# Moving half of the expert row sums from VectorE to ScalarE

## The chip, the cores and the metric

The kernel runs on one core of a Trainium2 chip. The metric is the device time of one execution in microseconds. TensorE does the matmuls (PE in the profile, its weight loads PEld), VectorE is DVE, ScalarE is ACT, GpSimd is POOL, and SyncE (SP) issues the plain weight transfers. Each has its own queue of instructions, worked off in order. They tell each other of finished work through semaphores.

## The reference, cut to what matters

The program is two layers over 256 tokens of width 1024, in float32. Each layer mixes tokens (a convolution, an attention and a state-space scan), attends to a memory, and ends in a feed-forward part that draws on a table of 16384 experts. The change touches that last part alone:

```python
# for each chunk of 128 tokens: 8 heads x 16 chosen experts per token
u_e = jnp.take(u_tab, expert, axis=0)
v_e = jnp.take(v_tab, expert, axis=0)
act = jax.nn.gelu(jnp.einsum('chkd,cd->chk', u_e, xc).astype(jnp.float32))
return jnp.einsum('chk,chkd->cd', (gate * act).astype(v_e.dtype), v_e)
```

So for each of 128 chosen experts of a token, a dot product of 1024 products (the `u` row with the token), a gelu, a gate factor, and a weighted sum of the `v` rows.

## The kernel before, in words

**Stages.** Tokens lie on the 128 partitions. There are four stages `ci`, two chunks of 128 tokens in each of two layers. The expert part of one stage overlaps with the mixing, memory attention and expert choice of the next. Experts are numbered `n` = 0 to 511, 128 in a stage. For each `n`, GpSimd issues one indirect gather (line 1145) that brings, for every token, the `u` row and the `v` row of one expert, 128 rows of 8 KB, into one of nine slots of `slots`. The `u` half is `slots[:, s, 0:D]`, the `v` half follows it.

**The path of one expert.** VectorE waits for the gather and makes the dot product (`dot_of`, line 2030): one instruction multiplies the `u` half by the token (`htok`), writes the products back into the slot, and adds them up into one column of `dot`; a second instruction reads the accumulator out. ScalarE takes two experts at a time (`gelu`, line 1534): it waits until both dots are there, makes one gelu of two columns, then two products with the gate (`coef`, line 1539), and then scales the identity by each coefficient (`diagonal`, line 1521). TensorE multiplies that diagonal with the `v` half, in two matmuls of 512 columns, and so adds the expert up in two PSUM banks (`add_expert`, line 1007). After the second matmul, the semaphore `slot_used` lets GpSimd gather the next expert into the slot. For 33 experts VectorE adds the `v` half up instead.

**What sets the order.** Every engine walks the same loop over ticks, one expert per tick from tick 100 on. All other work is written as strands, each piece with the tick at which it is issued. On ScalarE a tick does this in order: diagonals of the last pair (even `n`), strands of this tick, and on odd `n` the gelu of the pair `n-1, n`. VectorE's tick: the dot of `n`, then strands. TensorE runs two ticks behind. Different activation functions need a table load on ScalarE (ACT_TABLE_LOAD); it is put in front of the activation that needs it.

**Single experts.** The last four experts (`n` from `SINGLE` = 508) get a gelu each.

Of the kernel before, what the change touches and what calls it, by code (L numbers as in the profile page):

```python
# [10 lines left out]
ALU = mybir.AluOpType  # L11
ACT = mybir.ActivationFunctionType
# [5 lines left out]
D = 1024  # L18
# [13 lines left out]
PH, NK, TOP = 8, 128, 16  # L32
# [99 lines left out]
SINGLE = NG - 4  # L132
# [3 lines left out]
SLOT = [n % 7 for n in range(20)] + [(6, 8, 0, 1, 7, 2, 3, 4, 5)[n % 9] for n in range(NG - 20)]  # L136

USED = [SLOT[:n].count(SLOT[n]) for n in range(NG)]


def in_slot_before(n):

    return max(k for k in range(n) if SLOT[k] == SLOT[n])
# [7 lines left out]
def begun(pieces):  # L151

    return [[next(p, NEVER), p] for p in pieces]


def go_on(strands, tick):
    for s in strands:
        while s[0] <= tick:
            s[0] = next(s[1], NEVER)


def build(nc, x_d, mem_d, blocks_d, prm_d, rows_d, experts0_d, experts1_d, out_d):
    ctx = ExitStack()
    with ctx:
        def sb(name, shape, dt=F32):
            return ctx.enter_context(nc.sbuf_tensor(name, shape, dt))

        def sem(name):
            return ctx.enter_context(nc.semaphore(name))

        x = sb("x", [P, NC, D])
        slots = sb("slots", [P, SLOTS, 2 * D])
# [5 lines left out]
        htok = sb("htok", [P, 2, D])  # L178
# [71 lines left out]
        dot = sb("dot", [P, 2, TOP])  # L250
# [100 lines left out]
        gexp_ready = sem("gexp_ready")  # L351
        idx_ready = sem("idx_ready")
        dot_ready = sem("dot_ready")
        gelu_ready = sem("gelu_ready")
        gate_ready = sem("gate_ready")
        coef_ready = sem("coef_ready")
# [754 lines left out]
        def _(eng):  # L1111
# [17 lines left out]
            for n in range(NG):  # L1129
# [6 lines left out]
                s = SLOT[n]  # L1136
                if USED[n]:
                    before = in_slot_before(n)
# [12 lines left out]
        def _(eng):  # L1151
            act = nc.scalar.activation
# [15 lines left out]
            def root_ahead():  # L1168

                act(ahead[:, :], epsb[:, :], ACT.Sqrt)  # L1170
# [305 lines left out]
            def phasors(l):  # L1476
                at = BEGIN[l]
                for n, i in enumerate((1, 0)):
                    yield at + (15 + n if l == 0 else SETUP_TICK[1](ANGLE_OP[1]) + 1)
                    eng.wait_ge(angle_ready, 2 * l + n + 1)  # L1480
                    act(T[:, :, i, :], T[:, :, i, :], ACT.Sin, scale=TURN).then_inc(phasor_ready, 1)

            def gates():
                for q in range(NST * PH):
                    yield route_tick(q, BEST_OP) + (1 if q else 0)
                    j = q % 2
                    eng.wait_ge(best_ready, q + 1)
                    if q < len(HEADS[0]):
                        act(gexp[:, j, :], best[:, j, :], ACT.Exp, scale=rs0[:, :], bias=nbest[:, j, :],
                            accum_out=gsum[:, j, :]).then_inc(gexp_ready, 1)  # L1490
                        if q == 0:
                            act(ahead1[:, :], zero[:, :], ACT.Gelu_apprx_tanh)
                    else:
                        act(gexp[:, j, :], best[:, j, :], ACT.Exp, bias=nbest[:, j, :], accum_out=gsum[:, j, :])\  # L1494
                            .then_inc(gexp_ready, 1)

            def final(c):
                yield FINAL[c]
                root_ahead()
                for i in range(2):  # L1500
                    h = slice(i * 512, (i + 1) * 512)
                    eng.wait_ge(x_added, 2 * (NST - NC + c) + i + 1)
                    act(htok[:, 0, h], x[:, c, h], ACT.Square, accum_out=fss[:, i:i + 1]).then_inc(half_squared, 1)
                eng.wait_ge(half_squared, 2 * c + 2)
                eng.wait_ge(first_part, c + 1)
                act(root[:, :], fss[:, 1:2], ACT.Sqrt, scale=1.0 / D, bias=fpart[:, :]).then_inc(norm_root, 1)
                yield FINAL[c] + 2
                eng.wait_ge(final_rs, c + 1)
                b, n = turn[("gain", 1, ("final", c))]
                eng.wait_ge(emptied[b], n + 1)  # L1510
                act(outs[c][:, 512:], outs[c][:, 512:], ACT.Copy, scale=rs[:, :]).then_inc(out_right, 1)
                if c == NC - 1:
                    eng.wait_ge(out_right, c + 1)
                    nc.scalar.dma_start(out_d[c * P:(c + 1) * P, 512:], outs[c][:, 512:]).then_inc(stored, 16)

            def diagonal(n):
                q, k = divmod(n, TOP)
                i = TAKEN[n]
                if i >= DIAGS:
                    eng.wait_ge(slot_used, i - DIAGS + 1)  # L1520
                act(diag[:, i % DIAGS, :], ident[:, :], ACT.Copy, scale=coef[:, q % 2, k:k + 1])\  # L1521
                    .then_inc(diag_ready, 1)
# [5 lines left out]
            for l in range(L):  # L1528
                strands += [mem_keys(l), phasors(l)]
            strands = begun(strands + [gates()] + [final(c) for c in range(NC)])  # L1530
            def gelu(n, many):
                q, k = divmod(n, TOP)
                eng.wait_ge(dot_ready, n + many)
                act(gel[:, q % 2, k:k + many], dot[:, q % 2, k:k + many], ACT.Gelu_apprx_tanh).then_inc(gelu_ready, 1)  # L1534
                if k == 0:
                    eng.wait_ge(gate_ready, q + 1)
                eng.wait_ge(gelu_ready, n // 2 + 1 if many == 2 else SINGLE // 2 + n - SINGLE + 1)
                for i in range(k, k + many):
                    act(coef[:, q % 2, i:i + 1], gel[:, q % 2, i:i + 1], ACT.Copy, scale=gexp[:, q % 2, i:i + 1])\  # L1539
                        .then_inc(coef_ready, 1)  # L1540

            for tick in range(LAST):
                n = tick - G0
                if 2 <= n <= SINGLE and n % 2 == 0:
                    eng.wait_ge(coef_ready, n)
                    for k in (n - 2, n - 1):
                        if TAKER[k] == "tensor":
                            diagonal(k)
                if SINGLE < n <= NG:
                    eng.wait_ge(coef_ready, n)  # L1550
                    diagonal(n - 1)
                go_on(strands, tick)
                if 0 <= n < SINGLE and n % 2:
                    gelu(n - 1, 2)
                if SINGLE <= n < NG:
                    gelu(n, 1)

        @block.vector
        def _(eng):
            v = nc.vector  # L1560
# [464 lines left out]
            def dot_of(n):  # L2025
                q, k = divmod(n, TOP)
                ph = n // PER
                s = SLOT[n]
                eng.wait_ge(arrived[s], 16 * (USED[n] + 1))
                v.tensor_tensor_reduce(out=slots[:, s, 0:D], in0=slots[:, s, 0:D], in1=htok[:, ph % 2, :],  # L2030
                                       scale=1.0, scalar=0.0, op0=ALU.mult, op1=ALU.add,
                                       accum_out=dot[:, q % 2, k:k + 1]).then_inc(dot_ready, 1)
# [66 lines left out]
            for tick in range(LAST):  # L2099
                n = tick - G0  # L2100
                ph, m = divmod(n - PER - 2, PER)
                if m == 0 and 0 <= ph < NST:
                    add_to_x(ph)
                if 0 <= n < NG and n % TOP == 0:
                    gate_factor(n // TOP)
                if 0 <= n < NG:
                    dot_of(n)
                if 2 <= n <= NG + 1 and TAKER[n - 2] == "vector" and n % 2 == 0:
                    add_slot(n - 2)
                go_on(strands, tick)  # L2110
                go_on(route, tick)
                if 2 <= n <= NG and n % 2 == 0 and TAKER[n - 1] == "vector":
                    add_slot(n - 1)
# [7 lines left out]
def route_tick(q, n):  # L2121

    if q == 0:
        return 94
    if q == 1:
        return 97 + n * 3 // 4
    if q == PH * (NST - 1) or q % PH not in HEADS[q // PH]:
        return G0 + TOP * (q - 1) + 1 + (n - 1) // 2
    return G0 + TOP * (q - 1) - 6 + (n - 1)
# [78 lines left out]
```

## Time and profile before

| What | us |
|---|---|
| Median of the three runs | 1693.98 |
| The runs | 1693.75, 1693.98, 2640.91 |
| The profiled execution's own time | 1695.05 |
| Its span, first to last instruction | 1693.1 |
| Busy: TensorE 91%, VectorE 69%, ScalarE 43%, GpSimd 35% | |
| DMA over the span: 675.13 MB, mean 399 GB/s | |

The span is what the profile shows of one execution. A busy share is an average over stages that differ; what is worth something in one of them is read from that stretch. Idle time of an engine is put down to what ended it.

### The profile page before, as it was taken

What the parts mean: (1) busy time and instruction counts of PE and PEld (TensorE: products, weight loads), DVE (VectorE), ACT (ScalarE), POOL (GpSimd) and SP (SyncE); (2) the same over time, 40 slices, a digit from 0 to 9 for tenths busy, and PEclk for the clock granted to TensorE, in tenths of its full rate; (3) what the DMA queues carried; (4) which work ended last, traced back from release to release, by engine and by line L of the source; (5) the groups of instructions that cost most, each with busy time, mean ns of one, the idle gap of its engine ahead of it and who ended that gap; (6) DMA issues with size and microseconds to landing.
All of it is one profiled execution on the core that took longest, in us unless ns stands there. A gap on an engine that the chain in (4) does not pass through costs nothing.

```text
span 1693.1 us, 19218 instructions
## 1 busy us (share of the span) xinstructions
PE 1538.1 (91%) x6354; PEld 893.6 (53%) x6354; DVE 1170.7 (69%) x2955; ACT 734.0 (43%) x1963; POOL 595.9 (35%) x527
## 2 busy tenths in 40 slices
PE   9999999889999999988988889988999999777776
PEld 8757775347567656434645446434656554222232
DVE  7821899974877658986555667995556666666655
ACT  4142534763464333385433353465444334333333
POOL 0000454443333334343333343343343544344331
PEclk9999999999999999999999999999999999999999
DMA  9655999999999999999999999999999999999996
GB/s 384 258 201 221 381 416 421 421 422 420 421 420 420 421 414 421 420 419 421 420 421 421 411 421 421 380 416 412 421 410 419 421 420 421 421 422 421 421 421 285
DMA packets 94003, 675.13 MB, mean 399 GB/s; under 512 B 10424, under 2 KB 10704, under 8 KB 12496
## 3 DMA queue, kind: packets, MB, share of 16 engines
q0 software_dynamic: 73728, 536.90, 76.6%
q1 hardware_dynamic: 20032, 136.74, 20.0%
q8 instruction: 51, 0.84, 0.2%
q14 instruction: 48, 0.39, 0.1%
q10 hardware_dynamic: 144, 0.26, 0.0%
HBM read 672.81 MB, written 1.05 MB: 398 GB/s over the span
## 4 chain that ended last, share of the span: by engine, by line
PE 36%; DMA 34%; DVE 9%; ACT 5%; issue 2%; POOL 0%; DVEq 0%; ACTq 0%; POOLq 0%
DMA slots<-expert_rows,expert 34%; PE bank L1007 20%; PE bank L477 7%; DVE slots L2030 5%; PE bank L680 3%; PE bank L974 2%; PE bank L990 2%; ACT diag L1521 1%; ACT coef L1539 1%; ACT L1534 1%; PE bank L575 1%; PE bank L767 1%; PE bank L745 1%; ACT gel L1534 1%; DVE htok L1853 0%
## 5 line engine op out<-in xcount | busy, mean ns | idle before, releaser
L1007 PE MATMUL bank<-slots,diag 128*128 128x512 f32 x1914 | 899.7, 606 | 128.3 <-ACT diag L1521 121.5
L1145 POOL DMA_INDIRECT slots<-expert_rows,expert x512 | 593.9, 1160 | 1073.1 <-PE bank L1007 861.2
L2030 DVE CUSTOM_DVE_ANT_0 slots<-slots,htok 128x1024 f32<-128x1024 f32 x512 | 625.6, 1222 | 388.8 <-DMA slots<-expert_rows,expert 387.5
L1007 PEld LDWEIGHTS bank<-slots,diag 128*128 128x128 f32 x1914 | 345.4, 192 | 543.5 <-issue 321.7
L1534 ACT ACTIVATE gel<-dot 128x2 f32<-128x2 f32 (+1 forms) x258 | 52.5, 203 | 652.4 <-DVE dot L2030 651.7
L477 PEld LDWEIGHTS bank<-hT,ring 128*128 128x128 f32 x1488 | 180.6, 193 | 41.9 <-issue 40.4
L477 PE MATMUL bank<-hT,ring 128*128 128x128 f32 x1488 | 181.7, 276 | 1.4 <-ACT hT L1181 1.0
L1521 ACT ACTIVATE diag<-ident,coef 128x128 f32<-128x128 f32 x479 | 168.3, 394 | 8.8 <-PE bank L1007 0.4
L1539 ACT ACTIVATE coef<-gel,gexp 128x1 f32<-128x1 f32 x512 | 123.1, 287 | 10.4
L1534 ACT ACT_TABLE_LOAD x67 | 86.0, 1283 | 1.2
L1566 DVE SCALAR_TENSOR_TENSOR sg<-pad,prm,sg 128x128 f32<-128x128 f32 x240 | 71.5, 343 | 0.0
L680 PE MATMUL bank<-ring,hT 128*128 128x512 f32 x104 | 48.8, 598 | 1.0 <-issue 0.9
L1566 DVE SCALAR_TENSOR_TENSOR x<-slots,coef,x 128x1024 f32<-128x1024 f32 (+1 forms) x34 | 43.1, 1266 | 9.3 <-ACT coef L1539 9.2
L680 PE MATMUL bank<-ring,products 128*128 128x512 f32 x96 | 45.1, 592 | 0.0
L2030 DVE DVE_READ_ACCUMULATOR2_ANT dot<- 128x1 f32 x512 | 42.0, 82 | 0.0
L477 PEld LDWEIGHTS bank<-hT,slots 128*128 128x128 f32 x352 | 40.9, 192 | 2.1 <-issue 1.9
L477 PE MATMUL bank<-hT,slots 128*128 128x128 f32 x352 | 41.5, 275 | 0.3 <-DMA slots<-w_blocks 0.3
L477 PEld LDWEIGHTS bank<-hT,kept 128*128 128x128 f32 x256 | 31.6, 197 | 6.3 <-issue 6.3
L680 PEld LDWEIGHTS bank<-ring,hT 128*128 128x128 f32 x104 | 19.6, 193 | 26.1 <-issue 26.1
L1494 ACT ACT_TABLE_LOAD x25 | 32.1, 1283 | 0.4
L477 PE MATMUL bank<-hT,kept 128*128 128x128 f32 x256 | 31.7, 280 | 0.0
L536 PE MATMUL bank<-ring,hT 128*128 128x512 f32 x64 | 29.7, 592 | 0.0
(362 smaller groups left out, 1469.7 us busy)
## 6 DMA issues: line engine op xcount, KB each, us to landing
ring<-w_blocks SPq DMA_DIRECT2D x89, 1024.0 KB, 9.3
slots<-w_blocks SPq DMA_DIRECT2D x24, 1024.0 KB, 10.9
slots<-expert_rows,expert POOLq DMA_INDIRECT x512, 15.9
kept<-w_blocks SPq DMA_DIRECT2D x4, 1024.0 KB, 11.7
keys<-w_blocks SPq DMA_DIRECT2D x2, 1024.0 KB, 10.3
kv<-w_blocks SPq DMA_DIRECT2D x2, 1024.0 KB, 14.3
prm<-small SPq DMA_DIRECT2D x2, 768.0 KB, 12.9
x<-x_rows SPq DMA_DIRECT2D x2, 512.0 KB, 11.5
```

The costliest lines, as they stand in the source:

```text
L477: last = mm(bank[b][:, a * P:(a + 1) * P], w[:, k, a * P:(a + 1) * P], src[:, k, :], start=k == 0, stop=k == KT - 1)
L680: last = mm(bank[b + i][:, :], src[:, first + k, :], w[:, k, i * 512:(i + 1) * 512], start=start and k == 0, stop=stop and k == 1)
L974: last = mm(bank[b][:, a * M:(a + 1) * M], w[:, k, a * P:(a + 1) * P], memH[l][:, k, :], start=k == 0, stop=k == KT - 1)
L990: last = mm(bank[b][:, :], memH[l][:, t, m * P:(m + 1) * P], w[:, k, :], start=t == 0, stop=t == KT - 1)
L1007: last = mm(bank[h][:, :], diag[:, i % DIAGS, :], slots[:, SLOT[n], D + h * 512:D + (h + 1) * 512], start=m == 0, stop=n == end - (ph == N ...
L1145: nc.gpsimd.indirect_dma_start(slots[:, s, :], None, (experts0_d, experts1_d)[n // PER // NC], bass.IndirectOffsetOnAxis(ap=idx[q % 2][:, ...
L1494: act(gexp[:, j, :], best[:, j, :], ACT.Exp, bias=nbest[:, j, :], accum_out=gsum[:, j, :])\
L1521: act(diag[:, i % DIAGS, :], ident[:, :], ACT.Copy, scale=coef[:, q % 2, k:k + 1])\
L1534: act(gel[:, q % 2, k:k + many], dot[:, q % 2, k:k + many], ACT.Gelu_apprx_tanh).then_inc(gelu_ready, 1)
L1539: act(coef[:, q % 2, i:i + 1], gel[:, q % 2, i:i + 1], ACT.Copy, scale=gexp[:, q % 2, i:i + 1])\
L1566: return v.scalar_tensor_tensor(out=out, in0=in0, scalar=scalar, in1=in1, op0=op0, op1=op1)
L2030: v.tensor_tensor_reduce(out=slots[:, s, 0:D], in0=slots[:, s, 0:D], in1=htok[:, ph % 2, :], scale=1.0, scalar=0.0, op0=ALU.mult, op1=ALU.add,
```

## The change

Of each pair of experts that share a gelu, the first (even `n`, below 508, so 254 experts) is treated differently. VectorE only multiplies, with `tensor_tensor`, and writes the products into the slot. ScalarE then copies the 1024 products of each token onto themselves with an accumulator output, which puts their sum in the column of `dot`. A new semaphore `sum_ready` tells of it. The second expert of the pair and the last four are as before. The new step stands in ScalarE's tick `n`, behind that tick's strands; the strands of tick `n+1` and the pair's gelu come behind it.

```diff
+def summed_on_act(n):
+
+    return n % 2 == 0 and n < SINGLE
...
+            def sum_of_products(n):
+                q, k = divmod(n, TOP)
+                us = slots[:, SLOT[n], 0:D]
+                eng.wait_ge(dot_ready, n + 1)
+                act(us, us, ACT.Copy, accum_out=dot[:, q % 2, k:k + 1]).then_inc(sum_ready, 1)
+
             def gelu(n, many):
                 q, k = divmod(n, TOP)
+                if summed_on_act(n):
+                    eng.wait_ge(sum_ready, n // 2 + 1)
                 eng.wait_ge(dot_ready, n + many)
                 act(gel[:, q % 2, k:k + many], dot[:, q % 2, k:k + many], ACT.Gelu_apprx_tanh).then_inc(gelu_ready, 1)
...
                 go_on(strands, tick)
+                if 0 <= n < SINGLE and summed_on_act(n):
+                    sum_of_products(n)
                 if 0 <= n < SINGLE and n % 2:
                     gelu(n - 1, 2)
...
                 eng.wait_ge(arrived[s], 16 * (USED[n] + 1))
+                if summed_on_act(n):
+                    v.tensor_tensor(slots[:, s, 0:D], slots[:, s, 0:D], htok[:, ph % 2, :], ALU.mult)\
+                        .then_inc(dot_ready, 1)
+                    return
                 v.tensor_tensor_reduce(out=slots[:, s, 0:D], in0=slots[:, s, 0:D], in1=htok[:, ph % 2, :],
```

**ScalarE, around the softmax of a head's gates in the last stage.** In the rows, gexp is that softmax, gel and coef are the gelu and the coefficient, diag the scaled identity; brackets name the semaphores that a row waits for. Before:

```order
L1521 ACTIVATE diag<-ident,coef 128x128 [waits slot_used]
L1494 ACT_TABLE_LOAD
L1494 ACTIVATE gexp,gsum<-best,nbest 128x16 [waits best_ready]
L1534 ACT_TABLE_LOAD
L1534 ACTIVATE gel<-dot 128x2 [waits dot_ready]
L1539 ACTIVATE coef<-gel,gexp 128x1 [waits gelu_ready]
```

and with the change:

```order
L1527 ACTIVATE diag<-ident,coef 128x128 [waits slot_used]
L1500 ACT_TABLE_LOAD
L1500 ACTIVATE gexp,gsum<-best,nbest 128x16 [waits best_ready]
L1541 ACTIVATE slots,dot<-slots 128x1024 [waits dot_ready]
L1548 ACT_TABLE_LOAD [waits dot_ready]
L1548 ACTIVATE gel<-dot 128x2 [waits sum_ready]
L1553 ACTIVATE coef<-gel,gexp 128x1 [waits gelu_ready]
```

The new sum stands ahead of the gelu's table load. The gelu now has two waits, and one of them, for the second dot of the pair, sits on the table load. It is so at all 67 loads of the gelu's table, none of which waited before. ScalarE has as many table loads as before.

**VectorE, dots of four experts in the last stage.** Before:

```order
L2030 ISA slots,dot<-slots,htok 128x1024 [waits arrived0]
L2030 ISA dot 128x1
L2030 ISA slots,dot<-slots,htok 128x1024 [waits arrived1]
L2030 ISA dot 128x1
L2030 ISA slots,dot<-slots,htok 128x1024 [waits arrived7]
L2030 ISA dot 128x1
```

and with the change:

```order
L2047 TENSOR_TENSOR slots<-slots,htok 128x1024 [waits arrived0]
L2050 ISA slots,dot<-slots,htok 128x1024 [waits arrived1]
L2050 ISA dot 128x1
L2047 TENSOR_TENSOR slots<-slots,htok 128x1024 [waits arrived7]
L2050 ISA slots,dot<-slots,htok 128x1024 [waits arrived2]
```

Every second dot is one instruction where there were two; nothing else moves on VectorE.

## Rows read from the trace of the kernel before

**Rows 1.** The page: busy time by engine, and GB/s in 40 equal slices.

```profile
PE 1538.1 (91%) x6354; PEld 893.6 (53%) x6354; DVE 1170.7 (69%) x2955; ACT 734.0 (43%) x1963; POOL 595.9 (35%) x527
GB/s 384 258 201 221 381 416 421 421 422 420 421 420 420 421 414 421 420 419 421 420 421 421 411 421 421 380 416 412 421 410 419 421 420 421 421 422 421 421 421 285
```

**Rows 2.** Chain of work that ended last, shares by engine.

```profile
PE 36%; DMA 34%; DVE 9%; ACT 5%; issue 2%; POOL 0%; DVEq 0%; ACTq 0%; POOLq 0%
```

**Rows 3.** Five stretches: length, busy us by engine, TensorE's clock, DMA share, GB/s.

```profile
280.00:350.00 70.00, 63.07 (x234) 30.77 (x233) 62.85 (x151) 51.87 (x116) 29.83 (x24) 0.98 1.01 421
700.00:765.00 65.00, 57.91 (x208) 27.78 (x207) 59.08 (x150) 48.86 (x115) 29.31 (x24) 1.00 1.01 419
1090.00:1160.00 70.00, 59.92 (x230) 30.30 (x229) 59.42 (x145) 51.43 (x114) 26.93 (x23) 0.95 0.96 393
1160.00:1320.00 160.00, 158.42 (x666) 95.49 (x665) 97.69 (x231) 70.23 (x192) 63.45 (x55) 1.00 1.01 415
1440.00:1640.00 200.00, 147.63 (x320) 57.50 (x320) 131.62 (x319) 69.72 (x220) 78.02 (x80) 1.00 1.01 421
```

**Rows 4.** The expert gathers of the whole span, from issue to landing.

```profile
DMA to landing us min/median/max: 7.4/15.9/25.3
```

**Rows 5.** The same, of the gathers issued from 280 to 350 us.

```profile
DMA to landing us min/median/max: 9.9/13.5/20.8
```

**Rows 6.** The same, from 700 to 765 us.

```profile
DMA to landing us min/median/max: 13.2/15.3/22.2
```

**Rows 7.** The same, from 1160 to 1320 us.

```profile
DMA to landing us min/median/max: 10.3/13.5/19.1
```

**Rows 8.** Groups of instructions by form: busy us, mean ns of one, idle before.

```profile
L2030 DVE CUSTOM_DVE_ANT_0 slots<-slots,htok 128x1024 f32<-128x1024 f32 x512 | 625.6, 1222 | 388.8 <-DMA slots<-expert_rows,expert 387.5
L2030 DVE DVE_READ_ACCUMULATOR2_ANT dot<- 128x1 f32 x512 | 42.0, 82 | 0.0
L2018 DVE TENSOR_TENSOR cands<-cands,topi 128x512 f32<-128x512 f32 x31 | 21.3, 686 | 0.2
L1943 DVE TENSOR_TENSOR cands<-tops 128x256 f32<-128x256 f32 x32 | 13.0, 405 | 0.0
L1175 ACT ACTIVATE hT<-x 128x1024 f32<-128x1024 f32 x10 | 10.5, 1047 | 11.0 <-DVE x L1566 9.3 <-DMA x<-x_rows 1.4
L1175 ACT ACTIVATION_READ_ACCUMULATOR hT<-x 128x1 f32 x10 | 1.9, 186 | 0.0
L1323 ACT ACTIVATE hT<-x,rs 128x1024 f32<-128x1024 f32 x4 | 4.5, 1136 | 0.2 <-DVE rs L1687 0.2
L1534 ACT ACT_TABLE_LOAD x67 | 86.0, 1283 | 1.2
```

**Rows 9.** Waits over the whole span: total us, times, longest us.

```profile
ACT gel L1534 <- DVE dot L2030: 651.7, 207, 9.2
PE bank L1007 <- ACT diag L1521: 121.5, 101, 4.1
```

**Rows 10.** ScalarE's timeline in the last stage: start, us, what, [idle before].

```profile
1450.47 0.69 ACT L1521 ACTIVATE diag<-ident,coef 128x128 f32<-128x128 f32 x2
1451.18 1.28 ACT L1494 ACT_TABLE_LOAD   x1
1452.47 0.31 ACT L1494 ACTIVATE gexp<-best,nbest 128x16 f32<-128x16 f32 x1
...
1452.89 1.28 ACT L1534 ACT_TABLE_LOAD   x1
1454.62 0.20 ACT L1534 ACTIVATE gel<-dot 128x2 f32<-128x2 f32 x1 [0.45 <-DVE dot L2030]
```

**Rows 11.** TensorE's timeline around the same pair.

```profile
1455.82 3.70 PE L1007 MATMUL bank<-slots,diag 128*128 128x512 f32 x8 [1.20 <-ACT diag L1521]
1460.80 2.41 PE L1007 MATMUL bank<-slots,diag 128*128 128x512 f32 x5 [1.28 <-ACT diag L1521]
```

**Rows 12.** ScalarE's timeline in a stretch of attention.

```profile
1132.75 1.28 ACT L1534 ACT_TABLE_LOAD   x1
1134.17 0.20 ACT L1534 ACTIVATE gel<-dot 128x2 f32<-128x2 f32 x1
...
1139.01 1.28 ACT L1534 ACT_TABLE_LOAD   x1
1140.30 0.20 ACT L1534 ACTIVATE gel<-dot 128x2 f32<-128x2 f32 x1
```

**Rows 13.** Line 1534 alone, 1090 to 1160 us: its gelus and table loads.

```profile
1090.00:1160.00 70.00, 12.71 (x20) 0.95 0.96 393
```

More of the change, by code:

```diff
@@ L353, in build @@
         dot_ready = sem("dot_ready")
+        sum_ready = sem("sum_ready")
         gelu_ready = sem("gelu_ready")
```

## The prediction

> **What bounds the kernel now.** I read the page's slices first. From the fifth of forty slices to the last but one the core moves 410 to 422 GB/s in all but two (381 and 380) [rows 1]. Then the stretches: the DMA share is 1.01 at about 421 GB/s both where TensorE is nearly full (158.42 of 160 us) and where it is not (147.63 of 200 us) [rows 3]. So the transfers set the pace. The rate also explains the length: the last stage issues 80 gathers in 200 us, one per 2.50 us, and one gather is 128 rows of 8 KB, 1.05 MB, which takes 2.49 us at 421 GB/s. All 675.13 MB at 421 GB/s are 1604 us; most of the other 89 us of the span lies in the opening slices (258, 201, 221 GB/s) and in the last one (285), where the change touches little. The chain that ended last is 36% TensorE and 34% DMA [rows 2]: the two take turns, because a gather waits for a slot that TensorE frees, and an expert waits for its gather.
>
> The question is therefore how much later a slot may come free before the transfers run dry. A gather takes a median 15.9 us from issue to landing, against 2.49 us of transfer of its own, so some five others are ahead of it. The least is 7.4 us [rows 4]; I take that as the shortest queue that the trace shows. Above it there are 2.5 us at the thinnest point of 280 to 350 us (9.9) and 6.1 us at the median (13.5) [rows 5], 5.8 us at the thinnest from 700 to 765 [rows 6], and 2.9 us at the thinnest from 1160 to 1320 (10.3) [rows 7]. That is the cover of every delay below.
>
> **VectorE.** 254 times, 1222 + 82 ns of dot and accumulator read become one multiply. None of 1024 columns is in the trace. From 256 to 512 columns `tensor_tensor` goes from 405 to 686 ns, 1.10 ns a column, so 1024 columns give 686 + 562 = 1248 ns; the fused instruction's 1222 ns for the same columns is the other bound [rows 8]. I take 1235 ns. Saved: 1304 - 1235 = 69 ns each, 18 us in all (14 to 21). VectorE is 69% busy, and waits 388 us for the gathers in front of its dots [rows 8]: hidden, worth nothing to the end. Where it is full (62.85 of 70 us, 59.08 of 65) [rows 3] there are 12 pairs, so 0.8 us a stretch, below what I count.
>
> **ScalarE, the new sum.** The nearest row is the square of 128x1024 with an accumulator, 1047 + 186 = 1233 ns; a copy with a scale per partition takes 1136 ns and would make it 1322 [rows 8]. I take 1.23 us, since the copy has no such scale. 254 of them are 313 us: ScalarE goes from 734 to 1047 us, 62% of the span. Is it on the path? ScalarE waits 651.7 us for dots, 3.1 us each of 207 times [rows 9]. The sum of expert n starts when its products are there, and runs while VectorE makes the dot of n+1. That dot ends at least 1.3 us after the products, so the sum of 1.23 us is done when the second dot is. Cost in the quiet stretches: nothing. The cover is the dot; without it the sum would be 1.23 us on the way to the gelu.
>
> **ScalarE, the table load behind a wait.** The order shows what the diff does not: the 67 loads of the gelu's table now wait for the second dot. Before, the load ran while ScalarE waited for it: it ended at 1454.17 and the gelu began at 1454.62, after 0.45 us of idle time for the dot [rows 10]. Now it begins where the gelu began. So 67 pairs get their gelu 1.28 us later [rows 8]. In the attention stretches ScalarE is itself late (the load ends, the gelu follows at once, at 1134.17 and 1140.30 [rows 12]); there the load was in the open already, and the 1.23 us of the sum in front of it takes its place as the delay, up to 1.28 where the wait binds too. Either way about 1.28 us per load, 86 us in all if nothing hid it.
>
> What hides it? In the last stage TensorE has 3.70 us of matmuls in a round of 4.98 us, and waits 1.20 to 1.28 us for the diagonal [rows 11]. A gelu 1.28 us late makes it idle once for 2.5 us and lets the slots go 1.28 us late; the next round begins on time again. The queue of gathers is 15 us deep there. Cost: nothing. The same holds wherever loads are 40 us apart.
>
> **ScalarE full.** In the three attention stretches the loads are dense. Line 1534 has 20 instructions in 12.71 us [rows 13]: 8 loads of 1.283 and 12 gelus. So 12 sums come in, 14.8 us, and ScalarE's busy time goes to 66.7 of 70, 63.7 of 65 and 66.2 of 70 us [rows 3]. It also stands still where its order makes it wait. So the eight loads' 10.3 us can't all be made up. Neither end is shown: at the low end nothing gets through, since TensorE has 7 to 10 us of idle time per stretch [rows 3]; at the high end all 10.3 us do. I take half, 5.1 us of lateness per stretch, and set the queue against it. First stretch, against the median cover of 6.1 us, at the thinnest point 2.5: somewhere between 0 and 2.6, I take 0.9. Second: 5.8 us of cover, 0. Third: TensorE does not catch up in the 160 us behind it, where it is 99% busy, so the lateness stays until the thinnest point, 2.9 us: 2.2 us lost. Sum: 3.1 us.
>
> The strands of odd ticks now stand behind the sum as well. TensorE, which reads what they write, is two ticks behind, so this delay of at most 1.23 us per tick is inside the lateness taken.
>
> **A rule on table loads.** In rows 10 the load of 1.28 us begins at 1451.18, 0.02 us after the diagonals end, and the activation behind it starts 0.01 us after the load. The Trainium skill, "ScalarE: Activation LUTs", section "What ACT_TABLE_LOAD costs", says that a drain of about 1380 ns comes on top, 2.66 us for every switch. By that the 67 loads would cost 178 us, and the lateness per stretch would be 21 us. The trace has no such drain, so it does not enter the sum.
>
> **The rivals.**
> *ScalarE and the late loads become the bound (slower).* The place is the three attention stretches and the loads just before and behind them; the mechanism is the one above, but the lateness gets past the queue. For it: ScalarE at 95 to 98%, and TensorE's 121.5 us of waits for diagonals [rows 9]. Against it: 10 to 15 us of queued gathers. It decides from about 5 us of lateness per stretch on. If all of the 24 loads got through, 24 x 1.28 = 30.8 us less covers of 2.5, 5.8 and 2.9 give +20 us: 1714. If in these stretches the 36 sums were not hidden either, 44 us more: 1758. With all 67 loads on the path, and no sum, 1694 + 86 = 1780. The Trainium skill, same page, section "Rules for kernel authors", speaks for this rival: it gives add and mul to VectorE, not ScalarE; no row shows ScalarE that full.
> *The queue covers all of it (no change).* 1694. For it: the DMA share of 1.01 in four of the five stretches.
> *VectorE's relief counts (faster).* If the dots in the full stretches set the pace, 18 us saved at most: 1676. Against it: the DMA share there is as full as elsewhere.
> *The change does not do what it says.* That would be so if VectorE still summed the first row of a pair; the order shows one instruction there in place of two, so it is excluded.
>
> **How the numbers follow.** The sum is against the profiled execution, 1695.05 us (span 1693.1 and 1.95 around it); it is 1.07 above the median of 1693.98. 1695.05 + 3.1 - 1.07 = 1697. Chances: a small loss of 0 to 10 us with the queue as cover 0.74, of which the no-change case is a good third; a part of the late loads past the queue, 1704 to 1727, 0.16; ScalarE's lateness past 2%, 1728 or more, 0.07; faster by a few us through VectorE 0.03, of which 0.01 by more than 2%. Two per cent is about what a measurement of this kernel tells from no change. So faster 0.01, same 0.92, slower 0.07. For the range I leave out the last of the slower cases and what is below 1690, since the transfers can't be made up: 1690 to 1718.
>
> **What would show it.** The multiplies at 1.22 to 1.25 us and the sums at 1.23 us. Gelu loads that start at the end of the second dot, and gelus 1.28 us behind it. The DMA share at 1.01 from 1440 on, landings near 15 us with single ones 1.3 us shorter. In the attention stretches ScalarE above 90% busy and landings shorter by some 5 us, with a dip in GB/s near 1160 to 1310. Wrong would be: a DMA share well below 1 in several stretches (then the queue was no cover), or TensorE late in the quiet stages, which would mean that the sum is not hidden behind the second dot.

## The result, and the profile after

| | before | changed |
|---|---|---|
| Median of 22 runs, us | 1693.84 | 1696.40 |
| Lowest to highest, us | 1693.15 to 2640.91 | 1693.81 to 1698.29 |
| Span of the profiled execution, us | 1693.1 | 1694.1 |

The ratio is 1.0012, with a 95% interval of 1.0006 to 1.0017. The medians differ by 2.6 us, and the ratio stands for 2.0 us: a small loss, clear of zero, against a forecast of 1697 us (3.1 us of loss). One of the 22 executions before took 2640.91 us, and the ratio leaves it out as a slow one. The profiled executions lie closer together than the medians: the one before is 1.1 us above its median, the changed one 0.3 us below its own. So the rows show where time went, and the medians how much.

The page, to be held against [rows 1] and [rows 2]:

```profile
PE 1544.7 (91%) x6354; PEld 897.4 (53%) x6354; DVE 1166.7 (69%) x2701; ACT 1009.9 (60%) x2471; POOL 593.8 (35%) x527
GB/s 382 259 201 221 377 422 420 415 417 420 421 420 421 421 421 421 420 411 416 421 421 422 421 421 421 397 419 366 421 405 414 421 422 421 421 421 421 421 422 317
PE 43%; DMA 25%; ACT 10%; DVE 6%; issue 2%; POOL 0%; ACTq 0%; POOLq 0%
```

ScalarE went from 734 to 1010 us, VectorE only from 1171 to 1167. The core still moves 421 GB/s nearly everywhere. One slice stands out, the 28th (1143 to 1185 us): 366 where it was 412. In the chain ScalarE's share doubled, from 5% to 10%.

The groups by form (busy us, mean ns of one, idle before), beside [rows 8]:

```profile
L2047 DVE TENSOR_TENSOR slots<-slots,htok 128x1024 f32<-128x1024 f32 x254 | 310.1, 1221 | 174.6 <-DMA slots<-expert_rows,expert 174.3
L2050 DVE CUSTOM_DVE_ANT_0 slots<-slots,htok 128x1024 f32<-128x1024 f32 x258 | 315.3, 1222 | 169.1 <-DMA slots<-expert_rows,expert 168.5
L1541 ACT ACTIVATE slots<-slots 128x1024 f32<-128x1024 f32 x254 | 267.2, 1052 | 142.5 <-DVE slots L2047 142.5
L1541 ACT ACTIVATION_READ_ACCUMULATOR slots<-slots 128x1 f32 x254 | 48.0, 189 | 0.0
L1548 ACT ACT_TABLE_LOAD x67 | 86.0, 1283 | 30.7 <-DVE dot L2050 30.0
```

The multiply takes as long as the fused dot did (1221 against 1222 ns); only the 82 ns of the accumulator read are saved. Even they hardly relieve VectorE, whose busy time fell by 4 us and not by 254 times 82 ns, 21 us. In the kernel before, the read starts 0.07 us before the dot in front of it ends, and together with the next instruction, so it runs beside its neighbours:

```profile
1450.87 1.23 DVE L2030 CUSTOM_DVE_ANT_0 slots<-slots,htok 128x1024 f32<-128x1024 f32 x1 [0.86 <-DMA slots<-expert_rows,expert]
1452.03 0.08 DVE L2030 DVE_READ_ACCUMULATOR2_ANT dot<- 128x1 f32 x1
1452.03 0.09 DVE L1960 MATCH_VALUE_LOAD bestc<-best,cands 128x8 f32 x1
```

The sum takes 1052 + 189 ns. That is 315 us of instruction time, but the engine's busy time grew by 276: the read and the copy overlap by some 0.1 us. The table loads, which had 1.2 us of idle time before them, now have 30.7: they do wait for the second dot.

ScalarE's timeline in the last stage, beside [rows 10]:

```profile
1453.82 0.31 ACT L1500 ACTIVATE gexp<-best,nbest 128x16 f32<-128x16 f32 x1
1454.03 0.19 ACT L1500 ACTIVATION_READ_ACCUMULATOR gexp<-best,nbest 128x1 f32 x1
1454.12 1.04 ACT L1541 ACTIVATE slots<-slots 128x1024 f32<-128x1024 f32 x1
1455.07 0.19 ACT L1541 ACTIVATION_READ_ACCUMULATOR slots<-slots 128x1 f32 x1
1455.96 1.28 ACT L1548 ACT_TABLE_LOAD   x1 [0.70 <-DVE dot L2050]
1457.26 0.20 ACT L1548 ACTIVATE gel<-dot 128x2 f32<-128x2 f32 x1
```

The load begins when the dot has come, and the gelu follows it. TensorE around it, beside [rows 11]:

```profile
1452.27 3.70 PE L1013 MATMUL bank<-slots,diag 128*128 128x512 f32 x8 [1.30 <-ACT diag L1527]
1458.46 7.11 PE L1013 MATMUL bank<-slots,diag 128*128 128x512 f32 x12 [2.49 <-ACT diag L1527]
```

The wait of 2.49 us in place of 1.20 is the 1.28 us of the load. Yet the transfers do not feel it. The stretches (length, busy us by engine, TensorE's clock, DMA share, GB/s), beside [rows 3]:

```profile
280.00:350.00 70.00, 61.02 (x254) 30.96 (x249) 59.01 (x134) 59.31 (x130) 26.77 (x24) 0.98 1.01 415
700.00:765.00 65.00, 55.69 (x199) 26.75 (x198) 55.60 (x130) 55.48 (x126) 27.27 (x23) 0.97 1.01 414
1090.00:1160.00 70.00, 57.57 (x222) 29.71 (x220) 57.47 (x129) 59.01 (x128) 29.10 (x22) 0.92 0.99 401
1160.00:1320.00 160.00, 157.38 (x652) 94.38 (x652) 95.32 (x203) 99.42 (x247) 58.85 (x52) 0.99 0.98 403
1440.00:1640.00 200.00, 152.48 (x323) 59.73 (x321) 132.53 (x281) 114.82 (x300) 81.83 (x81) 0.97 1.01 421
```

From 1440 on the rate is 421 as before. From 1160 to 1320 it falls from 415 to 403: 12/421 of 160 us are 4.6 us of transfer time. The queue there got thin. From issue to landing, the gathers of 1160 to 1320 us, beside [rows 7]:

```profile
DMA to landing us min/median/max: 5.9/9.9/15.5
```

The median went from 13.5 to 9.9 us and the least from 10.3 to 5.9, below the 7.4 of [rows 4].

**The place.** First the 20 us from 1160, before the change, with the clock, DMA share and GB/s at the end of the row, then what precedes them on GpSimd and on TensorE:

```profile
1160.00:1180.00 20.00, 20.00 (x75) 11.07 (x74) 12.63 (x20) 4.28 (x13) 6.93 (x7) 1.00 0.99 402
```

```profile
1159.36 0.94 POOL L1145 DMA_INDIRECT slots<-expert_rows,expert  x1 [10.76 <-PE bank L1007]
1153.73 1.94 PE L921 MATMUL bank<-ident,htok 128*128 128x128 f32 x8 [3.07 <-ACT groot L1308]
```

Then the same with the change:

```profile
1160.00:1180.00 20.00, 20.00 (x68) 10.78 (x68) 11.35 (x15) 6.86 (x16) 6.63 (x6) 0.93 0.80 322
```

```profile
1162.83 0.94 POOL L1151 DMA_INDIRECT slots<-expert_rows,expert  x1 [10.89 <-PE bank L1013]
1157.20 1.94 PE L927 MATMUL bank<-ident,htok 128*128 128x128 f32 x8 [4.11 <-ACT groot L1314]
```

In both kernels GpSimd stands still for almost 11 us, since no slot comes free. TensorE waits there for `groot`, the square roots of the group norm, on ScalarE: 3.07 us before, 4.11 after.

The gap is as long as before but begins 3.3 and ends 3.5 us later, at the end of a stretch of attention in which ScalarE had little slack: from 1120 to 1157 us it is busy for 34.9 of 37 us, where it was 30.0. Before, then after:

```profile
1120.00:1157.00 37.00, 29.26 (x114) 14.74 (x114) 30.48 (x68) 29.98 (x68) 12.60 (x11) 0.94 1.01 421
1120.00:1157.00 37.00, 27.97 (x110) 13.33 (x108) 28.96 (x59) 34.91 (x78) 14.67 (x12) 0.98 1.01 413
```

So the gap meets a shorter queue, and the DMA share falls to 0.80: 99/421 of 20 us are 4.7 us without transfers, against 0.9 us before.

### The profile page after: what moved, and what is told of

It reads as the page before. It is cut to its first block, busy times and chain, and to the rows that moved or that the text cites. A ratio compares the mean times of both kernels' runs of the same rounds, so it can differ in the third digit from the quotient of the medians.

```text
span 1694.1 us, 19726 instructions
## 1 busy us (share of the span) xinstructions
PE 1544.7 (91%) x6354; PEld 897.4 (53%) x6354; DVE 1166.7 (69%) x2701; ACT 1009.9 (60%) x2471; POOL 593.8 (35%) x527
## 4 chain that ended last, share of the span: by engine, by line
PE 43%; DMA 25%; ACT 10%; DVE 6%; issue 2%; POOL 0%; ACTq 0%; POOLq 0%
DMA slots<-expert_rows,expert 25%; PE bank L1013 24%; PE bank L483 9%; PE bank L686 3%; DVE slots L2050 3%; ACT L1548 2%; PE bank L980 2%; PE bank L996 2%; ACT diag L1527 1%; ACT coef L1553 1%; ACT slots L1541 1%; DVE slots L2047 1%; ACT gel L1548 1%; PE bank L773 1%; PE bank L751 1%
## 5 line engine op out<-in xcount | busy, mean ns | idle before, releaser
L2050 DVE CUSTOM_DVE_ANT_0 slots<-slots,htok 128x1024 f32<-128x1024 f32 x258 | 315.3, 1222 | 169.1 <-DMA slots<-expert_rows,expert 168.5
L2047 DVE TENSOR_TENSOR slots<-slots,htok 128x1024 f32<-128x1024 f32 x254 | 310.1, 1221 | 174.6 <-DMA slots<-expert_rows,expert 174.3
L1541 ACT ACTIVATE slots<-slots 128x1024 f32<-128x1024 f32 x254 | 267.2, 1052 | 142.5 <-DVE slots L2047 142.5
L1548 ACT ACT_TABLE_LOAD x67 | 86.0, 1283 | 30.7 <-DVE dot L2050 30.0
L686 PE MATMUL bank<-ring,hT 128*128 128x512 f32 x104 | 48.6, 596 | 1.0 <-issue 0.9
L1541 ACT ACTIVATION_READ_ACCUMULATOR slots<-slots 128x1 f32 x254 | 48.0, 189 | 0.0
```

The costliest lines, as they stand in the source:

```text
L686: last = mm(bank[b + i][:, :], src[:, first + k, :], w[:, k, i * 512:(i + 1) * 512], start=start and k == 0, stop=stop and k == 1)
L1541: act(us, us, ACT.Copy, accum_out=dot[:, q % 2, k:k + 1]).then_inc(sum_ready, 1)
L2047: v.tensor_tensor(slots[:, s, 0:D], slots[:, s, 0:D], htok[:, ph % 2, :], ALU.mult)\
```

## The experiments

Each is compared with the kernel before, run beside it. Ratios have their 95% interval; differences are of medians. Those below 1 us are not told from zero here. Theories A, B and C are named in the expectation of the first experiment in which they stand.

**e1, the gelu's two waits in the other order.**

```diff
+                eng.wait_ge(dot_ready, n + many)
                 if summed_on_act(n):
                     eng.wait_ge(sum_ready, n // 2 + 1)
-                eng.wait_ge(dot_ready, n + many)
```

> The two waits of the gelu change places in the code, so that the table load carries the wait for the sum and the gelu the wait for the second dot; all else is the changed kernel. Theory A (the loss of 2 to 2.5 us comes from the gelu's table loads, that start only behind the second dot, where the queue of gathers is thin): the loads move back by up to 1.28 us wherever ScalarE was not late already, and the loss shrinks by a half or more: 0 to 1.2 us over the kernel before. Theory B (the loss comes from the sum's own 1.23 us on a ScalarE that is full in the attention stretches): nothing changes, 2 to 2.5 us over. In the last stage the first theory and the second both expect TensorE's wait at a load to fall from 2.5 to about 1.3 us.

Measured: 1696.26 against 1693.77 us, ratio 1.0014 (1.0005 to 1.0023). The load now starts before the dot has come:

```profile
1452.48 1.04 ACT L1541 ACTIVATE slots<-slots 128x1024 f32<-128x1024 f32 x1
1453.42 0.19 ACT L1541 ACTIVATION_READ_ACCUMULATOR slots<-slots 128x1 f32 x1
1453.69 1.28 ACT L1548 ACT_TABLE_LOAD   x1
```

Then TensorE at that pair, and the group of loads over the whole run:

```profile
1456.18 3.70 PE L1013 MATMUL bank<-slots,diag 128*128 128x512 f32 x8 [1.86 <-ACT diag L1527]
L1548 ACT ACT_TABLE_LOAD x67 | 86.0, 1283 | 4.0
```

The dot's accumulator is read at 1454.21. TensorE's wait at that pair is 1.86 us, where it was 2.49 and both theories had about 1.3: the sum in front of the load takes up half of what the wait gives back. Over the whole run the idle time in front of the 67 loads falls from 30.7 to 4.0 us. The loss stays 2.5 us, so the loads' wait for the dot is not its cause.

**e2, sums in the attention stretches only; e3, everywhere else.**

```diff
-    return n % 2 == 0 and n < SINGLE
+    return n % 2 == 0 and n < NG - PER and 32 <= n % PER < 60          # e2
+    return n % 2 == 0 and n < SINGLE and not (n < NG - PER and 32 <= n % PER < 60)   # e3
...
```

In these two, and in e9 and e10, the gelu's wait counts only the sums that are made.

> ScalarE sums only 42 of the 254: those with n % 128 from 32 to 59 of the first three stages, the attention stretches. Both A and B: nearly the whole loss, 1.5 to 2.5 us over the kernel before. Theory C (the loss is made in the quiet stretches, many small delays): 0 to 0.5 us.

> The complement: ScalarE sums the 212 that lie outside the attention stretches. A and B: 0 to 0.7 us over the kernel before. C: 1.5 to 2.5 us.

Measured: e2 1693.46 us, ratio 0.9999 (0.9990 to 1.0008); e3 1692.93 us, ratio 0.9995 (0.9986 to 1.0004), both against 1693.77. Neither half costs anything. A and B had e2 wrong, C had e3 wrong. Two parts that each cost nothing and together 2.6 us are what a cover would do that one part leaves in place. That reading is argued here; e5 to e10 test it. In e2 TensorE's wait at line 927 is as in the changed kernel (4.11 us for groot), but it ends at 1155.32 and not at 1157.20 us, and 1160 to 1180 us runs at 367 GB/s; in e3 the wait is 3.07 us, and the rate 424 GB/s:

```profile
1160.00:1180.00 20.00, 20.00 (x75) 11.15 (x74) 12.62 (x19) 6.31 (x19) 7.22 (x7) 1.00 0.91 367
```

```profile
1160.00:1180.00 20.00, 18.95 (x71) 10.29 (x69) 11.25 (x18) 8.74 (x20) 7.42 (x7) 1.00 1.01 424
```

**e4, the sum made short.**

```diff
-                us = slots[:, SLOT[n], 0:D]
+                us = slots[:, SLOT[n], 0:16]
```

> The copy on ScalarE takes 16 of the 1024 columns, so its output lacks the rest of the sum of the first row of each pair; the instruction stays in its place with its waits, at about 0.2 + 0.2 us in place of 1.24. A: the loads still stand behind the second dot; half or more of the loss stays, 1 to 2.5 us over. B: the loss goes, 0 to 0.5 us over, or a little below, since VectorE is relieved.

Measured: 1692.84 against 1693.77 us, ratio 0.9993 (0.9984 to 1.0002). The copy takes 211 ns in place of 1052, all waits are in their place, and 1160 to 1180 us runs at 420 GB/s:

```profile
L1541 ACT ACTIVATE slots<-slots 128x16 f32<-128x16 f32 x254 | 53.6, 211 | 156.4 <-DVE slots L2047 156.3
L1548 ACT ACT_TABLE_LOAD x67 | 86.0, 1283 | 70.3 <-DVE dot L2050 69.7
```

```profile
1160.00:1180.00 20.00, 20.00 (x74) 10.86 (x72) 11.84 (x19) 7.07 (x22) 6.62 (x6) 1.00 1.01 420
```

The loss is gone, though the loads wait for the second dot more than ever, 70.3 us in all. It is the sum's length. A short copy also moves less data to and from the slots, so one could think of the traffic instead. The rows speak against it: with full sums the core moves 421 GB/s from 1440 to 1640 us as before, and the multiplies take 1221 ns with full sums and 1223 with short ones.

**e5 to e8, a shallower queue.** A gather also waits until TensorE has used one (e5, e6) or two (e7, e8) experts more; e5 and e7 are the kernel before, e6 and e8 the changed one. Each was run four times.

```diff
                     eng.wait_ge(slot_used if TAKER[before] == "tensor" else slot_added, TAKEN[before] + 1)
+                    if before + 1 < n:      # + 2 in e7 and e8
+                        later = max(k for k in range(before, before + 1 + 1) if TAKER[k] == "tensor")\
...
+                            eng.wait_ge(slot_used, TAKEN[later] + 1)
```

> The kernel before, but a gather into a slot also waits until TensorE has used the expert that follows the slot's last one: one gather less is under way, about 2.5 us of cover less. The theory that the queue of gathers is the cover: little lost here, since the thinnest queue of the kernel before still had 2.5 us above the shortest seen: 0 to 6 us over the kernel before.

> The changed kernel with the same hold. If the queue is the cover, the price of the change grows: 5 to 15 us over the held kernel before (e5), where it is 2.5 us without the hold. If the 2.5 us come from elsewhere (a fixed cost behind the last gather, the sum's own work), the difference stays 2 to 3 us.

> The kernel before with a hold of two experts, about 5 us less cover. Queue theory: the thin places run dry, 10 to 30 us over the kernel before.

> The changed kernel with a hold of two experts. Queue theory: 10 to 30 us over the held kernel before (e7). Fixed cost: 2 to 3 us over it.

| Hold | before, us | changed, us | difference | ratios to the kernel before |
|---|---|---|---|---|
| none | 1693.84 | 1696.40 | 2.6 | 1; 1.0012 |
| one expert | 1701.94 | 1710.65 | 8.7 | 1.0054 (1.0037 to 1.0070); 1.0088 (1.0070 to 1.0107) |
| two experts | 1717.40 | 1740.31 | 22.9 | 1.0144 (1.0128 to 1.0161); 1.0267 (1.0248 to 1.0285) |

By the ratios, the differences are 2, 6 and 21 us. With one expert held the two intervals just touch, with two they are far apart. The same work on ScalarE costs nine to ten times as much when two gathers less are under way. From the fifth slice to the last but one, the page of e8 has 25 of 35 below 418 GB/s, where the kernel before has 8:

```profile
GB/s 384 242 213 216 348 300 422 361 407 405 420 412 394 415 420 415 421 379 412 413 421 421 407 417 422 412 389 364 421 396 409 420 414 406 414 416 413 414 422 336
```

So the queue is the cover; a fixed cost would have stayed 2 to 3 us. The held kernel before lost more than expected at one expert (8.1 us, not 0 to 6): its cover was thinner than I had it.

**e9, no sums from expert 288 to 375; e10, only there.**

```diff
+    return n % 2 == 0 and n < SINGLE and not 288 <= n < 376       # e9
+    return n % 2 == 0 and 288 <= n < 376                          # e10
...
```

> ScalarE sums 210 of the 254, all but the 44 of experts 288 to 375, which are on the engines from about 1070 to 1325 us: the third attention stretch and the stretch behind it in which TensorE is full. Place theory (the loss is made there): 0 to 0.7 us over the kernel before, or below it. Rival (many small losses all over): 1.5 to 2.5 us over.

> The complement: only those 44 are summed on ScalarE. Place theory: 1.5 to 3 us over the kernel before. Rival: 0 to 0.7 us over.

Measured, against 1694.08 us: e9 1692.25, ratio 0.9991 (0.9982 to 1.0000); e10 1696.91, ratio 1.0013 (1.0004 to 1.0022). The 44 sums of experts 288 to 375 cost as much as all 254, the other 210 nothing. Of these 44, e2 had 14 and e3 the other 30, and neither share cost anything alone. The 20 us from 1160, e9 and then e10:

```profile
1160.00:1180.00 20.00, 20.00 (x75) 11.05 (x73) 11.86 (x23) 6.00 (x16) 6.60 (x6) 1.00 1.01 418
```

```profile
1160.00:1180.00 20.00, 20.00 (x69) 10.69 (x68) 11.19 (x15) 7.21 (x17) 6.62 (x6) 0.94 0.81 331
```

**e11, the sum behind the strands of the odd tick.**

```diff
-                if 0 <= n < SINGLE and summed_on_act(n):
-                    sum_of_products(n)
                 if 0 <= n < SINGLE and n % 2:
+                    sum_of_products(n - 1)
                     gelu(n - 1, 2)
```

> The sum stands behind the strands of the odd tick, directly in front of its gelu. If those strands, kept back by the sum's wait for VectorE, are what makes TensorE late: the loss shrinks to 0 to 1 us. If it is the sum's length on the way to the gelu: 2 to 5 us over, since the sum now starts later or at the same time.

Measured: 1698.09 against 1694.08 us, ratio 1.0026 (1.0017 to 1.0035), a loss of 4.0 us. The strands that the sum keeps back were not the matter; starting it later, up against the gelu, costs some 1.4 us more than the change did in its own comparison, with intervals that just touch.

**e12, the burden without the relief.** VectorE's new branch is taken out, so it keeps the fused dot for all, and ScalarE sums as in the change.

```diff
-                if summed_on_act(n):
-                    v.tensor_tensor(slots[:, s, 0:D], slots[:, s, 0:D], htok[:, ph % 2, :], ALU.mult)\
-                        .then_inc(dot_ready, 1)
-                    return
```

> VectorE keeps the fused dot of every expert, and ScalarE copies and adds up all the same, so the sum of each first row is made twice. It has the change's burden on ScalarE without the relief of VectorE. If the relief is worth nothing: as the changed kernel, 2 to 3 us over the kernel before. If it is worth its 20 us in the full stretches in part: 4 to 8 us over.

Measured: 1694.89 against 1694.08 us, ratio 1.0007 (0.9998 to 1.0016). VectorE's relief is worth nothing: without it the kernel is no slower than with it. That it should be quicker than the change by 1.8 us is not settled, since the intervals overlap; its rate from 1160 to 1180 us is 367 GB/s, between the two.

**The place in the runs without a hold.** ScalarE's busy time just ahead of the gap, and the rate around it, from the one profiled execution of each:

| Kernel | us over the kernel before | ScalarE busy, 1120 to 1157 us | GB/s, 1090 to 1320 us |
|---|---|---|---|
| before | 0 | 30.0 | 409 |
| e9, e4, e3 | -1.8, -0.9, -0.8 | 29.9, 29.8, 29.7 | 413, 411, 409 |
| e2, e12, e1 | -0.3, 0.8, 2.5 | 33.2, 34.0, 33.8 | 406, 403, 404 |
| changed, e10, e11 | 2.6, 2.8, 4.0 | 34.9, 34.9, 34.9 | 402, 400, 401 |

From 170 to 1090 us all of them move 417 or 418 GB/s. So the loss goes with a full ScalarE and a lower rate at this one place. Within the middle row the traces don't say why e1 loses 2.5 us and e2 nothing: from 1160 to 1180 us, e1 moves 372 GB/s and e2 only 367.

No version beat the kernel before clearly. e9 is the nearest, at the edge of its interval.

## Why the prediction was right

**The bound** was read rightly: transfers at 421 GB/s, in a kernel whose engines' lateness counts only when the queue of gathers runs low. e5 to e8 show it.

**The relief of VectorE**, taken as 18 us and worth nothing: 1221 ns a multiply gave 83 ns each, 21 us of instruction time but 4 us of busy time, since the read ran beside its neighbours. e12 shows that they don't reach the end.

**The new sum**, taken as 1.23 us and 313 us in all, took 1.24 us and 315. In the quiet stretches it is behind the second dot, as forecast: e3 loses nothing with 212 sums there. ScalarE's busy time in the three attention stretches was forecast as 66.7, 63.7 and 66.2 us. It came to 59.3, 55.5 and 59.0. That term was too large in two ways: 11 sums take 12.6 us of busy time, for 12 at 14.8, and in a stretch which runs late 5 to 6 us less of ScalarE's other work passes. So two signs that the forecast named did not come: ScalarE was 84 to 85% busy there, not above 90, and the median landing of the first two stretches fell by 1.6 and 2.5 us, not by some 5.

**The step that failed is the share of the table loads.** I said that about 1.28 us per load come late, because the load waits for the second dot, and made the lateness of a stretch out of eight loads. The mechanism exists (30.7 us of idle time in front of the loads, 2.49 us of wait on TensorE). But e1 takes nearly all of the idle time away and nothing changes, and e4 keeps it and the loss goes. At the place itself there was little to take away: from 1090 to 1160 us the changed kernel's loads wait for the dot twice, 1.3 us in all, for eight loads priced at 1.28 each. What makes the stretch late is the sum's own 1.24 us on a ScalarE that has little idle time there (2.1 of the 37 us from 1120 on): between the attention's pieces and the load, where ScalarE is late already, the sum is simply in line. I had named this ("the 1.23 us of the sum in front of it takes its place as the delay") and then priced both alike. Of the two gelus read there as starting at once [rows 12], the first starts 0.14 us after its load's end, so at that pair ScalarE was not late.

**The covers.** First stretch, taken as 0.9 us: 415 against 421 GB/s over 70 us, 1.0 us. Second, taken as 0: 414 against 419 over 65 us, 0.8 us. But slices between the stretches give this back (the 15th and the 23rd, 414 and 411 GB/s before, 421 after), and from 170 to 1090 us both kernels move 418 GB/s (where one GB/s is 2.2 us). Third, with what lies behind it, taken as 2.2: 401 against 393 over 70 us gives back 1.3, and 403 against 415 over 160 us takes 4.6, so 3.3. So the 0.9 us of the first stretch has no counterpart in the end time that could be told: e9 and e10 put all of it that is measurable in the third. The 2.2 us there were half of eight loads' 10.3 us less a cover of 2.9, and those loads are not what costs. That 3.1 us came so near to 2.6 is luck in its size; that a small loss comes through at the third stretch was reasoned. The reason named for that place, that TensorE is 99% busy behind it and the lateness stays, fits, but no run tests it alone. What I had not seen is the event around which the lateness counts: the 10.8 us without a gather around the group norm, which was in the trace of before. Once the gathers run, the next longest such gap there is 8.5 us, up to 895 us.

**The rivals.** The slower one had the right mechanism in part (ScalarE full, the lateness past the queue), and e8 shows it in force, with a queue two gathers shorter. Its point was put at about 5 us of lateness; 3.5 us were enough for a partial loss at the thinnest place. By the rule of the Trainium skill, "ScalarE: Activation LUTs", section "What ACT_TABLE_LOAD costs", that a drain of about 1380 ns comes on top of each table load, 21 us of lateness per stretch would have come. In these rows an activation starts 0.02 us behind the end of its load (1455.96 + 1.28, then 1457.26), so the measurement decides against the rule here.

## What to carry to other kernels

In a kernel bound by transfers, count how much later a buffer may come free before the queue is empty, place by place, and look for the longest gap between two issues: here a change cost what it took from the queue ahead of that gap, beyond what the queue could spare. Moving half of a fused instruction to another engine relieves the first only by what the fused form cost above the plain one, here 83 of 1304 ns by the rows and some 16 ns each in busy time, while the other pays 1241 (some 1090 in busy time). Two parts of a change that cost nothing alone can cost together, so a bisection by halves can come out empty.

## What the runs showed that was not expected

TensorE's clock fell after longer waits. In the last stage the granted clock was 1.00 over 200 us before and 0.97 after. At the wait of 2.49 us it looks so (clock, DMA share and GB/s last):

```profile
1455.00:1460.00 5.00, 2.51 (x6) 0.81 (x5) 3.25 (x7) 3.96 (x10) 1.40 (x2) 0.96 1.01 421
1460.00:1465.00 5.00, 5.00 (x10) 2.13 (x9) 3.69 (x6) 2.53 (x7) 1.33 (x2) 0.70 1.01 419
1495.00:1500.00 5.00, 2.52 (x6) 0.87 (x5) 3.25 (x7) 3.75 (x9) 1.18 (x2) 1.00 1.01 421
1500.00:1505.00 5.00, 5.00 (x12) 2.01 (x11) 3.68 (x6) 2.53 (x7) 3.43 (x3) 1.00 1.01 421
```

In the 5 us behind the wait a part was at 1.2 in place of 2.4 GHz (0.70 on the mean), with 10 matmuls; at the next such wait, 40 us on, the clock stayed at 1.00, with 12. So the drop follows only some of these waits. It cost nothing here: TensorE is idle a quarter of that stage, and the rate stays 421 GB/s. From 1160 to 1180 us, where it does count, the clock was 0.93 after and 1.00 before, and TensorE did 68 matmuls in 20 busy us in place of 75. No run holds the clock fixed, so its share of the 2.6 us is open. The traces speak against a large one. Over the 60 us from 1140 the clock is 0.94 on the mean in both kernels, since before it was low ahead of 1160 (0.83 from 1140 on, against 0.90). e1 has 1.00 and 74 matmuls from 1160 to 1180 us and loses 2.5 us all the same; e3 has 0.97 from 1090 to 1320 us, as the changed kernel, and loses nothing.
